# High and low input rows side by side in one 512-column product per weight block

## The reference, cut to what matters

```
h = rms_norm(x); proj = h @ w_in                    # 1024 x 7696
a, b, c = short_conv, retention, gated linear attention of parts of proj
merged = sum over the 3 of sigmoid(gate_i) * (y_i @ w_branch_i)      # 512 x 1024 each
x = x + rms_norm(merged @ w_out)                    # 1024 x 1024
h = rms_norm(x)
x = x + rms_norm((silu(h @ w_gate) * (h @ w_up)) @ w_down)   # 1024 x 2816, 2816 x 1024
```

```
u = dwconv3(h @ w_up) ; a, g = split(u)             # 1024 x 5632, a convolution over 3 tokens
x = x + g2 * ((a * silu(g)) @ w_down)               # 2816 x 1024
```

## Time and profile before

| | |
|---|---|
| median of 3 runs | 3027.86 us (3027.72 to 3030.34) |
| profiled execution, its own time | 3016.1 us |
| its span | 3014.3 us, mean granted clock 0.973 |
| TensorE busy | 94% of the span |
| GpSimd, VectorE, ScalarE busy | 50%, 45%, 44% |

### The profile page before, as it was taken

One profiled execution on the slowest core, in us unless ns is written; L12 is line 12 of the kernel. 1 busy time (PEld: TensorE's weight loads), 2 busy tenths in 40 slices (PEclk: granted clock), 3 DMA queues, 4 the chain that ended last, 5 costly groups with the idle time before them and its releaser, 6 DMA issues.

```text
span 3014.3 us, 44357 instructions
## 1 busy us (share of the span) xinstructions
PE 2825.6 (94%) x18084; PEld 2430.0 (81%) x18084; DVE 1349.9 (45%) x2106; ACT 1333.7 (44%) x2130; POOL 1505.3 (50%) x628
## 2 busy tenths in 40 slices
PE   7999999989999979989999989899998999998999
PEld 6889899888889977756777767688887868887999
DVE  5665411366551137943533432432335745446433
ACT  5464544545554443444233323342334554334554
POOL 4567578556757753311232324344444424445687
PEclk9999999999999999989999999999998989999999
DMA  5457775434777542211121213223332312223454
GB/s 189 133 191 244 236 235 192 133 119 158 260 247 252 176 133 84 77 35 36 53 67 49 84 50 98 70 96 101 98 98 93 106 47 98 88 95 119 147 182 161
DMA packets 144879, 386.60 MB, mean 128 GB/s; under 512 B 11824, under 2 KB 64304, under 8 KB 144688
## 3 DMA queue, kind: packets, MB, share of 16 engines
q1 hardware_dynamic: 144688, 383.87, 38.7%
HBM read 382.77 MB, written 1.05 MB: 127 GB/s over the span
## 4 chain that ended last, share of the span: by engine, by line
issue 35%; PE 32%; POOL 27%; DVE 4%; ACT 1%; POOLq 0%; DMA 0%; DVEq 0%; ACTq 0%
POOL w_lo L921 27%; PE bank L962 9%; PE bank L963 8%; PE bank L964 8%; PE bank L1309 1%; DVE sd L1715 1%; PE bank L1279 1%; PE bank L1028 1%; PE bank L995 1%; PE bank L1246 1%; PE bank L1231 1%; DVE bank L2094 0%; PE bank L984 0%; PE bank L983 0%; PE bank L982 0%
## 5 line engine op out<-in xcount | busy, mean ns | idle before, releaser
L921 POOL TENSOR_TENSOR w_lo<-raw,w_hi 128x1024 fp32r<-128x1024 f32 x624 | 1505.1, 2419 | 1498.0 <-ACT w_hi L1340 1497.0
L962 PE MATMUL bank<-h_hi,w_hi 128*128 128x256 f32 (+1 forms) x3456 | 1127.5, 326 | 78.8 <-DVE h_lo L2020 31.6
L963 PE MATMUL bank<-h_lo,w_hi 128*128 128x256 f32 (+1 forms) x3456 | 1097.9, 318 | 0.0
L964 PE MATMUL bank<-h_hi,w_lo 128*128 128x256 f32 (+1 forms) x3456 | 1097.2, 317 | 0.0
L1340 ACT ACTIVATE w_hi<-raw 128x1024 fp32r<-128x1024 f32 x624 | 655.2, 1054 | 398.8 <-PE bank L964 285.4
L962 PEld LDWEIGHTS bank<-h_hi,w_hi 128*128 128x128 f32 x3456 | 669.4, 194 | 172.8 <-issue 76.6
L963 PEld LDWEIGHTS bank<-h_lo,w_hi 128*128 128x128 f32 x3456 | 671.9, 194 | 42.6 <-issue 4.1
L964 PEld LDWEIGHTS bank<-h_hi,w_lo 128*128 128x128 f32 x3456 | 670.5, 194 | 40.7
L962 PE MATMUL bank<-hid_hi,w_hi 128*128 128x256 f32 (+1 forms) x704 | 218.2, 310 | 0.0
L963 PE MATMUL bank<-hid_lo,w_hi 128*128 128x256 f32 (+1 forms) x704 | 217.9, 309 | 0.0
L964 PE MATMUL bank<-hid_hi,w_lo 128*128 128x256 f32 (+1 forms) x704 | 217.9, 309 | 0.0
(11 more groups left out here) (273 smaller groups left out, 3522.2 us busy)
## 6 DMA issues: line engine op xcount, KB each, us to landing
raw<-stream SPq DMA_DIRECT2D x624, 512.0 KB, 3.4
spare_lo<-stream SPq DMA_DIRECT2D x32, 512.0 KB, 5.3
mix<-stream SPq DMA_DIRECT2D x32, 512.0 KB, 5.6
spare_hi<-stream SPq DMA_DIRECT2D x32, 512.0 KB, 5.7
xs<-x_rows SPq DMA_DIRECT2D x4, 256.0 KB, 4.1
xs<-ctx_rows SPq DMA_DIRECT2D x1, 1024.0 KB, 14.3
out_rows<-xs SPq DMA_DIRECT2D x8, 128.0 KB, 2.2
cst<-consts SPq DMA_DIRECT2D x1, 896.5 KB, 10.6
```

The costliest lines, as they stand in the source:

```text
L921: nc.gpsimd.tensor_tensor(w_lo[:, unit % SPLIT, :], raw[:, unit % RAW, :], w_hi[:, unit % SPLIT, :], ALU.subtract).then_inc(lo_ready, 1)
L962: nc.tensor.matmul(acc, wh, x_hi[:, k, c0:c1], start=k == 0, stop=False)
L963: nc.tensor.matmul(acc, wh, x_lo[:, k, c0:c1], start=False, stop=False)
L964: last = nc.tensor.matmul(acc, wl, x_hi[:, k, c0:c1], start=False, stop=k == t.k - 1)
```

## The change

`product_halves` takes the place of `product` in the products that run on 256 columns from the gates of the first block on: gates, branches, w_out and the whole feed-forward part of both layers of the first block, and w_out and the feed-forward part in the last layer of the second block. The high and the low input rows are made one tensor (`hl`, `y1`, `hid`, `hid2`, with a dimension for high and low), so that one product of the high weight takes both, 2 x 256 = 512 columns, and fills a whole bank: high by high in columns 0 to 255, high by low in 256 to 511. The low weight's product adds to columns 0 to 255. So a block has two matmuls (512 and 256 columns) where it had three of 256. These blocks are per layer of the first block 24 x 8 (gates), 24 x 4 (branches), 8 x 8 (w_out), 44 x 8 and 8 x 22 (feed-forward), 880, twice; and in the last layer 8 x 8, 44 x 8, 16 x 11, 592: 2352 in all.

Whoever takes such a tile has to add the two halves of its bank. VectorE does so with a sum over an inner dimension of two (`add_halves`, a reduction that writes 256 values), 216 times in the first block and 44 times for the up-projection of the last layer; in `add_gated` it adds the two halves in two multiply-adds, the second of which waits for the first. ScalarE then works on the sum (`on_sum`, `square_rows`), no longer on the bank. The second factor of each product goes to one fixed place, `half_sum`, in bank 6. These tiles rotate over the three banks 0, 1 and 3 (THREE): before it was two in the first block and seven in the last layer, where the sums now lie in banks 4 to 7. The sums of `ada_w` have two banks instead of three, and one of its units moves from before the feed-forward part into it.

```diff
+            def product_halves(x, c0, c1, count=1, fresh=None, more=1):
+                for i_tile in range(count):
+                    t, n, b = TILES[at["tile"]], PLACE.first_out[at["tile"]], PLACE.first_block[at["tile"]]
+                    acc = bank_of(n)
+                    for k in range(t.k):
...
+                        if k:
+                            nc.tensor.matmul(acc[:, 0:SEQ], wl, x[:, 0, k, c0:c1], start=False, stop=False)
+                        last = nc.tensor.matmul(acc[:, :], wh, x[:, :, k, c0:c1], start=k == 0, stop=k == t.k - 1)
+                        if not k:
+                            last = nc.tensor.matmul(acc[:, 0:SEQ], wl, x[:, 0, k, c0:c1], start=False, stop=False)
...
+            if t.name in ("fa", "fg", "fd") and t.layer == DEPTH - 1:
+                pool = THREE
+            if t.name in ("ffg", "ffu") or t.array in ("w_branch_a", "w_branch_b", "w_branch_c") or (t.array, t.name) == ("w_in", "gate"):
+                pool = THREE
...
+            def on_sum(rows, func, scale, done):
+                n = next_tile()
+                E.later(tile_done, 1)
+                act.wait_ge(tile_out, n + 1)
+                nc.scalar.activation(rows, rows, func, scale=scale).then_inc(done, 1)
...
+            def both_halves(acc):
+                return acc[:, :].rearrange("p (s n) -> p n s", n=SEQ)
+
+            def add_halves(dst):
+                n = E.later(tile_out, 1) - 1
+                dve.wait_ge(tile_done, n + 1)
+                V.reduce_sum(dst, both_halves(banks[PLACE.bank[n]]), AX_X).then_inc(tile_out, 1)
+                return n + 1
...
                 for b in range(3):
                     for f in range(KD):
-                        E.need(tile_out, 2)
-                        g, y, p = gate1[:, f % 2, :], branch1[:, f % 2, :], prod1[:, f % 2, :]
+                        g = gate1[:, f % 2, :]
+                        add_halves(g)
+                        C.settle()
+                        if b == 2 and f:
+                            dve.wait_ge(merged_rows, KD * l + f)
+                        dve.wait_ge(tile_out, add_halves(half_sum))
+                        E.need(gate1_ready)
                         if b == 0:
-                            V.scalar_tensor_tensor(mix[:, f, SEQ:T2], g, 1.0, y, ADD, MUL).then_inc(merge_used, 1)
+                            mixed[f] = C.do(V.scalar_tensor_tensor(mix[:, f, SEQ:T2], g, 1.0, half_sum, ADD, MUL))
...
                             for j in range(2):
-                                bank = banks[PLACE.bank[PLACE.first_out[first_tile + 2 * t + j]]]
-                                y, u = by_stream(fc[:, b, j, cols]), by_stream(bank[:, cols])
+                                if l < DEPTH - 1:
+                                    n = E.later(tile_out, 1) - 1
+                                    rows = banks[PLACE.bank[n]][:, :]
+                                else:
+                                    rows = banks[SUMS_G[t % len(SUMS_G)] if j else SUM_A][:, 0:SEQ]
+                                    n = E.later(tile_out, 1) - 1
+                                    dve.wait_ge(tile_done, n + 1)
+                                    C.do(V.reduce_sum(rows, both_halves(banks[PLACE.bank[n]]), AX_X))
+                                    C.settle()
+                                    dve.sem_inc(sum_ready, 1)
+                                    dve.sem_inc(tile_out, 1)
+                                y, u = by_stream(fc[:, b, j, cols]), by_stream(rows)
```

More of the change, by code:

```diff
@@ L944, in bank_of, with product @@
                 return banks[PLACE.bank[n]]
-            def product(x_hi, x_lo, c0, c1, count=1, fresh=None, late=None, more=1):
+            def product(x, c0, c1, count=1, fresh=None, late=None, more=1):
                 for i_tile in range(count):
@@ L2030, in add_gated @@
                     dve.wait_ge(tile_done, n + 1)
[L2031 to L2034 removed]
+                    for i in range(2):
+                        acc = slice(i * SEQ, (i + 1) * SEQ)
+                        stream = i if l < DEPTH - 1 else 1
+                        part = slice(stream * SEQ, (stream + 1) * SEQ)
+                        last = V.scalar_tensor_tensor(xs[:, f, part], banks[PLACE.bank[n]][:, acc],
+                                                      mod[:, l, part_of_mod * KD + f, stream:stream + 1], xs[:, f, part], MUL, ADD)
+                        if l == DEPTH - 1 and i == 0:
+                            C.do(last)
+                            C.settle()
                     last.then_inc(tile_out, 1)
@@ L2294, in _ @@
                             last.then_inc(fc_rows, 1)
-                            gate_bank.append(bank)
+                            gate_rows2.append(rows)
                         if 1 <= t <= FF_HALF:
```

231 lines of the change are left out of this document (125 added, 106 removed).

## The result

The changed kernel is slower: 3036.78 us (median of 8 runs, 3031.72 to 3040.6) against 3028.53 us (8 runs, 3019.75 to 3032.62) for the kernel before. The ratio is 1.0029, 95% interval 1.0017 to 1.0041. The forecast was 3012 and faster, its own range 2999 to 3022. The profiled execution took 3036.35 us, its span 3034.3 at a mean clock of 0.965; before it was 3016.1, 3014.3 and 0.973.

What follows compares the result with a forecast made beforehand. TensorE's matmul starts were taken as the bound; -31.4 + 9.0 + 0.6 + 3.1 + 2.8 = -15.9 us on 3016.1 gave 3000.2, a factor of 0.9947, so 3012 us on the median; own range 2999 to 3022, upwards to 3038 with rivals.

Steps and rivals of the forecast that it cites:

- norms: Behind w_out and w_down: the reduction comes first, so the root starts 0.7 us later, 1.0 for the last; 3.1 us lost.
- 2352 blocks: All changed products: each block loses one matmul and its fixed 13.3 ns, 31.4 us saved.
- gates to w_out, two layers: First block's gates, branches and w_out: waits at the first pairs, 9.0 us, and first w_out tiles, 0.6 us, lost.
- feed-forward parts of the first block: First block's feed-forward: VectorE needs about 2.7 of TensorE's 5.55 us per pair, so no loss in steady state.
- last layer, from its w_out: Second block's last layer: two-step additions, 0.52 us twice, and later `hid2` rows, 0.9 us per half; 2.8 us lost.
- The gain: TensorE's spacing in changed blocks: 360 ns become 346.7 ns, no cost for the two-run input; 31.4 us saved.
- Rival 1: VectorE's reductions are slow from their stride and become the bound: up to 33 us more, 3045 us; chance 0.13.
- first w_out tile: Last input rows take about 2.8 us, TensorE has 2.4 us of other rows; 0.6 us lost for both layers.
- The first pairs: First gate and branch pairs: TensorE waits 7.5 us for late reductions, about 3 us of old waits go; net 4.5 per layer.
- rival 3: First pairs cost twice as much through blocked weight splits, or the clock falls to 1.2 GHz; 3022 to 3034; chance 0.09.
- `ada_w` units: Loads and sums of these units: nothing gained or lost, with two banks enough for their sums.
- The signs of being wrong: Anywhere changed: a reduction over 0.9 us, 512-column starts 240 ns apart, or TensorE waiting after each pair.

Runs made afterwards that it cites:

- e1: Changed kernel with high and low rows side by side for two inputs, so their 512 columns are one run; 3035.2 us, ratio 1.0039 to the kernel before.
- e2: Changed kernel with only the head norm's reciprocal after pairs 1 and 3, scaling and gating behind the next pair's reductions; 3019.42 us, ratio 0.9991 to the kernel before.
- e13: e9b_low_later with the second head-norm reciprocal behind the next gate's reduction, plus 30 useless 512-column products near 1209 us; 3027.73 us, one execution.
- e9b_low_later: e2 with low parts of the last two retention and four attention heads moved behind pairs six to eight; 3015.77 us, ratio 0.9975 to the kernel before.

## Why the prediction was wrong

The forecast was 3012 in a range of its own up to 3022; the measured 3036.8 is held only by the wider range up to 3038, which takes in the rivals, and the direction was the other one. By its terms, in us against the profiled execution of before. "Measured" is the change of the stage above (norms: the gap between last and first product, before 16.47, 16.47, 16.47 and 28.09, after 18.53, 17.33, 18.35 and 29.44; the gap behind the last w_out, 7.25 and 7.70, counts with the last layer), with the gain of its blocks taken out at 10.5 ns:

| term | predicted | measured |
|---|---|---|
| 2352 blocks | -31.4 | -24.7 |
| gates to w_out, two layers | +9.6 | +20.9 |
| feed-forward parts of the first block | 0 | +5.2 |
| norms | +3.1 | +6.1 |
| last layer, from its w_out | +2.8 | +3.5 |
| code that is not changed | 0 | +9.0 |
| sum | -15.9 | +20.0 |

- **The gain** had the right mechanism and was too large: "3 x 120.0 = 360 ns become 120.0 + 226.7 = 346.7 ns" measured 349.5. The value lies between the two bounds for the two-run input, but the cause is not the input's break (e1).
- **VectorE's reductions** were right: 676 to 700 ns in all 216 and 689 to 700 in the 44 of the last layer, so a neighbour half a bank away costs what an adjacent one does. Rival 1 falls. In the steady state VectorE is never late, as forecast; the first w_out tile waits 0.2 us for it in the first layer and nothing in the second, where 0.3 each were forecast (its own 2.8 less 2.4 would make 0.4).
- **The first pairs** are the step that failed: "Net 4.5 per layer: 9.0 us". The two layers lost 10.7 and 10.2 us. Its walk found most of the places and nearly the waits (7.5 us against 8.2 and 9.6), though 1.4 and 1.0 us of them are for a load that it put at nothing. It took off 3 us for the waits of before, which are 2.4. So the waits grew by 6 and 7 us and not by 4.5. The other 4.7 and 3 us it left out altogether. The clock falls to 1.2 GHz for some 10 us in the first layer and 4 in the second, worth at most 5 and 2 us; in e2 it doesn't. And ScalarE, stopped behind the reductions, then splits two units at once and makes a 0.75 us pair of low parts 4.9 us long, which is part of the waits. That is rival 3, at 0.09, by both of its routes, and the time is above even its range of 3022 to 3034, since the unchanged code comes on top. e2 shows that the queue order carries it: undoing it brings back 0.4 to 0.5% in time and 11 us in these two stages.
- **The norms** were mis-sized, by half. The root does come later, but by 1.9 us behind w_out (4.23 us after the last product begins, where it was 2.36) and not 0.7. The last additions of squares (L1780, two tiles in SBUF) stand behind the last reduction and beside a run of GpSimd, 1.96 us at 339.24, and TensorE's two sum matmuls follow them, where before they were hidden under ScalarE's table load.
- **The `ada_w` units** ("nothing is gained or lost") cost 1.67 us at 366.82, where a unit waits for VectorE's copy out of one of now two banks, and the moved unit about 0.5, both in the first layer. The half us is an estimate, and the rest of the 5.2 us I can't place.
- **The last layer** had nearly the right sum by luck: the waits for `hid2` that were forecast are not there, two for low weight parts, 1.0 us together and the longer at 2908.83, are.
- **Unchanged code.** No term was set for it. It is shown that the clock makes it, with the same work and waits, that kernels which are not late have it too (e13). The kernel before, too, has runs that are 9 us longer at a lower clock. That part of it cancels in the medians, where the two kernels are 8 and not 20 us apart, is argued from the spread of before's runs (3015.9 to 3032.6 us over all), not shown: its profiled execution, 3016.1 us at 0.973, is one of the runs at a high clock.
- **The signs of being wrong** did not come up: reductions stayed under 0.9 us, the 512-column starts at 236 ns came near to 240 without reaching it, and TensorE didn't wait after each pair. None of them looked at the clock, where the failed step shows.

## What to carry to other kernels

An operation that frees a buffer for the busiest engine must not stand behind long work of its own engine's queue: put the release first and the norm, the reciprocal and the low parts behind it. Before moving the take-out to another engine, walk that queue at its worst place, not in the steady state, and then ask what the engine that now waits (here ScalarE, then GpSimd) will do in a burst afterwards. When TensorE's work is shortened by under 1%, a few waits that let its clock fall weigh as much as the gain, and so does what the clock does in code that nobody touched; compare the stages of the same code first, with their clock, and time more than one execution.

The best version by the ratio, e9b_low_later, keeps the change and is 0.25% faster than the kernel before, 0.5% faster than the changed one.

## What I had not expected of the hardware

- The same code with the same waits took 56.5 or 59.6 us (clock 0.94 or 0.89), and 670 us of it up to 8.8 us more or less, between executions.
- Two subtractions of SBUF tiles on VectorE took 0.75 us alone and 4.9 us beside a double run of GpSimd.
- 512 columns from two places cost no more than from one: 236 ns both.
- 512 + 256 columns took 349.5 to 350.8 ns in either order, 3 to 4 ns more than the two widths apart; the cause is open.
